# Moving the subtraction of the weights' low parts from GpSimd to VectorE in a two-block transformer kernel

## The reference, cut to what matters

```
h = rms_norm(x)
q, k, v, g_ret, x_lru, y_lru, gate_ret, gate_lru = split(h @ w_in)        # w_in is 1024 x 7168
o  = head_group_norm(retention(rotary(q), rotary(k), v))                  # 4 heads
ya = (o * silu(g_ret)) @ w_ret_o
xc = causal_conv4(x_lru)
hl = scan(a * h + b),  a, b from sigmoid(xc @ w_r), sigmoid(xc @ w_i)     # RG-LRU
yb = (hl * gelu(y_lru)) @ w_lru_o
x  = x + (sigmoid(gate_ret) * ya + sigmoid(gate_lru) * yb) @ w_out
gate, val = split(rms_norm(x) @ ffn_w_up)                                 # 2 x 3072
x  = x + (gelu(causal_conv3(gate)) * val) @ ffn_w_down
out = rms_norm(x)
```

## Time and profile before

| | |
|---|---|
| median of 3 runs | 982.43 us |
| profiled execution, first to last instruction | 979.2 us |
| mean granted TensorE clock | 0.982 |
| TensorE matmul busy | 907.7 us, 93% |
| weight load busy | 831.9 us, 85% |
| VectorE busy | 465.1 us, 47% |
| ScalarE busy | 370.2 us, 38% |
| GpSimd busy | 519.6 us, 53% |
| GpSimd's low parts | 632 instructions, 481.3 us |
| VectorE's low parts | 10 instructions, 14.0 us |

### The profile page before, as it was taken

How to read it: one execution, slowest core, us unless ns; L and a number is a source line. 1 busy time by engine, 2 the same in 40 slices (tenths; PEclk the granted TensorE clock), 3 DMA queues, 4 the chain that set the end, 5 groups by cost and what they waited for, 6 DMA issues and landing times.

```text
span 979.2 us, 15689 instructions
## 1 busy us (share of the span) xinstructions
PE 907.7 (93%) x6134; PEld 831.9 (85%) x6134; DVE 465.1 (47%) x957; ACT 370.2 (38%) x678; POOL 519.6 (53%) x658
## 2 busy tenths in 40 slices
PE   5798998999999999999999999799999998999995
PEld 5797887888888776788989999798988998899894
DVE  4774577613588788712693266301112353232132
ACT  4345554212101144604344774253112343443441
POOL 4567562100011000203899589993340798999992
PEclk9899999999999899999999999899999999999999
DMA  9353330443443611221645344452623365555551
GB/s 348 99 167 121 111 130 31 167 146 131 132 169 130 258 44 45 86 102 29 229 152 159 121 179 145 145 178 100 223 65 129 109 192 156 189 179 189 179 186 44
DMA packets 37785, 139.38 MB, mean 142 GB/s; under 512 B 4304, under 2 KB 4432, under 8 KB 37456
## 3 DMA queue, kind: packets, MB, share of 16 engines
q1 hardware_dynamic: 37424, 136.90, 41.6%
q10 hardware_dynamic: 288, 1.48, 0.4%
HBM read 137.32 MB, written 1.05 MB: 141 GB/s over the span
## 4 chain that ended last, share of the span: by engine, by line
PE 49%; POOL 25%; DVE 11%; issue 9%; ACT 3%; DMA 2%; SPq 0%; DVEq 0%; ACTq 0%; POOLq 0%
POOL w_lo L2182 24%; PE psum L530 21%; PE psum L531 8%; PE psum L532 7%; PE psum L533 7%; DMA early<-in_early 2%; POOL rstd L2189 1%; PE psum L681 1%; DVE y_lo L1483 1%; PE psum L663 1%; ACT logits L1165 1%; DVE h_rows L1640 1%; PE psum L605 1%; PE psum L798 1%; DVE neg_max L1741 1%
## 5 line engine op out<-in xcount | busy, mean ns | idle before, releaser
L2182 POOL TENSOR_TENSOR w_lo<-raw,w_hi 128x256 fp32r<-128x256 f32 x632 | 481.3, 803 | 114.5 <-ACT w_hi L1077 112.4
L530 PE MATMUL psum<-first 128*128 128x256 f32 (+1 forms) x960 | 214.4, 380 | 4.9 <-ACT first L1115 2.2
L2189 POOL TENSOR_TENSOR rstd<-mean_sq,minus_half 128x8 f32<-128x8 f32 (+4 forms) x21 | 38.0, 1809 | 340.2 <-DVE mean_sq L1500 340.2
L1077 ACT ACTIVATE w_hi<-raw 128x1024 fp32r<-128x1024 f32 x168 | 172.1, 1055 | 111.8 <-DMA raw<-in_blocks 83.9
L531 PE MATMUL psum<-h_hi,w_hi 128*128 128x256 f32 x704 | 202.4, 288 | 12.8 <-POOL w_lo L2182 11.1
L530 PEld LDWEIGHTS psum<-first 128*128 128x128 f32 x960 | 178.1, 191 | 30.1 <-ACT first L1115 2.6
L532 PE MATMUL psum<-h_lo,w_hi 128*128 128x256 f32 x704 | 200.9, 285 | 0.0
L533 PE MATMUL psum<-h_hi,w_lo 128*128 128x256 f32 x704 | 200.8, 285 | 0.0
L531 PEld LDWEIGHTS psum<-h_hi,w_hi 128*128 128x128 f32 x704 | 136.9, 194 | 15.7 <-issue 14.3
L532 PEld LDWEIGHTS psum<-h_lo,w_hi 128*128 128x128 f32 x704 | 137.0, 195 | 0.1
L533 PEld LDWEIGHTS psum<-h_hi,w_lo 128*128 128x128 f32 x704 | 136.8, 194 | 0.0
(11 more groups left out here) (266 smaller groups left out, 1108.2 us busy)
## 6 DMA issues: line engine op xcount, KB each, us to landing
raw<-in_blocks SPq DMA_DIRECT2D x168, 512.0 KB, 3.5
first<-in_blocks SPq DMA_DIRECT2D x64, 512.0 KB, 4.4
w_late<-in_blocks SPq DMA_DIRECT2D x20, 512.0 KB, 4.4
early<-in_early SPq DMA_DIRECT2D x1, 1579.0 KB, 14.8
attention<-in_late ACTq DMA_DIRECT2D x1, 1376.0 KB, 6.9
rows<-in_mem SPq DMA_DIRECT2D x2, 512.0 KB, 4.4
x<-in_x SPq DMA_DIRECT2D x1, 1024.0 KB, 8.5
out_x<-h_rows SPq DMA_DIRECT2D x2, 512.0 KB, 2.6
```

The source lines that it names most:

```text
L530: return nc.tensor.matmul(out, lhs[0], rhs[0], start=start, stop=stop, skip_group_check=shared_bank)
L1077: nc.scalar.activation(split_part(w_hi, q), raw[:, q % RAW_SLOTS, :], ACT.Copy).then_inc(w_hi_ready, 1)
L2182: ins = nc.gpsimd.tensor_tensor(lo[:, at], full[:, at], hi[:, at].bitcast(F32), ALU.subtract)
L2189: rstd_ready.mark(nc.gpsimd.tensor_tensor(rstd[:, n % 2, 0:width], mean_sq[:, n % 2, 0:width], minus_half[:, 0:width], ALU.pow), name, pool)
```

## The change

VectorE takes the low parts of all halves from index 19 on, each in two instructions of 1024 columns. To do so, `split_to` on VectorE calls `own_low_parts` where it only counted before. Three calls of `split_to` in its program are added or moved, and GpSimd's wait for `head_centred` goes. GpSimd keeps the low parts of twelve halves of layer 0, of halves 16, 17 and 18, and all roots.

```diff
-VECTOR_LO = [("b_k", 1), ("m_qg0", 0), ("m_qg0", 1), ("b_v", 1), HALVES[-1]]
+VECTOR_FROM = len(L0_SPLIT) + SPLIT_SLOTS
+VECTOR_LO = [("b_k", 1), ("m_qg0", 0), ("m_qg0", 1), ("b_v", 1)] + HALVES[VECTOR_FROM:]
...
             def split_to(n):
 
-                split[0] = max(split[0], min(n, len(HALVES)))
+                while split[0] < min(n, len(HALVES)):
+                    j = split[0]
+                    split[0] += 1
+                    if j >= VECTOR_FROM:
+                        own_low_parts(HALVES[j])
...
             link(ins)
+            split_to(proj.after[("r_v1", 1)] + LEAD)
             for f in range(KT):
                 ins = V.tensor_tensor_scan(xc(f), tile_of(0, f), tile_of(3072, f), 0.0, ALU.mult, ALU.add)
...
             retention_gate(1, 1)
-            split_to(proj.after[("g_ret0", 1)] + LEAD + 2)
-            r = scale_from("gn", sumsq[:, 0:T * RET_HEADS], S)
+            mean_from("gn", sumsq[:, 0:T * RET_HEADS], S, 1.0)
+            split_to(proj.after[("gate_r0", 0)] + LEAD)
+            r = root_of("gn", P)
...
             link(ins)
+            split_to(proj.after[("gate_r0", 1)] + LEAD)
             normed.mark(V.tensor_tensor(h_rows[:, :, :], h_rows[:, :, :], rows[:, :, 2048:3072], ALU.mult), "g_ret", vec)
...
             split_to(len(HALVES))
-            own_low_parts(HALVES[-1])
...
                     for q in (2 * j, 2 * j + 1):
-                        if q == 2 * half_index[("gate_r0", 0)] + 1:
-
-                            pool.wait_ge(head_centred, 1)
                         pool.wait_ge(w_hi_ready, q + 1)
```

## The result

The changed kernel takes 959.62 us (median of 4 runs, 959.36 to 959.67) against 982.42 us (980.4 to 983.42): ratio 0.9769, interval 0.9756 to 0.9783. The forecast was 961.7 us, with a range of 957 to 973. The profiled execution took 959.64 us and its span is 957.8, 1.8 us less.

What follows compares the result with a forecast made beforehand. TensorE, busy 93%, was taken to lose 21.8 us in block 2, nearly all behind GpSimd's subtractions. Gains 5.3 + 8.8 + 6.6 = 20.7 gave span 958.5, plus 3.2 to the median: 961.7 us, range 957 to 973.

Steps and rivals of the forecast that it cites:

- A: Block 2, c16 to c26: takes 68.8 us where 11 halves need 63.5; 5.3 us back.
- FFN: Block 2's FFN, 759.5 to 970.25 us: takes 210.75 us where matmuls need 204.1; 6.6 us back.
- the scan: VectorE's eight scans in B, left at their old duration, 8.7 us; at 0.48 each, 5.4 us less.
- B: Block 2, c31 to c43 with retention matmuls: takes 91.3 us for 81.4; 8.8 back, 9.9 less 1.1.
- new stop: In B after c33: TensorE wants `decayed(2)` at 590.25 us, VectorE ends it at 591.4; 1.1 us lost.
- the root of the group norm: GpSimd's root beside `lo(38)` in B: could wait for two VectorE subtractions, 2.4 us, leaving the sum the same.
- Retention as VectorE's chain: Rival in B: low parts before tight banks and slow centring make banks late; B gives back 4, 966.5 us; chance 0.20.
- The FFN loop: Rival: convolution, GELU, high and low part pace the FFN; each step stops 0.9 us or more, 967 us; chance 0.08.
- The loads: Rival: landing of `raw` loads, not low parts, sets the stops; only the FFN gains, 975.8 us; chance 0.04.
- Slower, the convolution slow of itself: Rival: block convolution stays 13.2 us, low parts 1.5 each; A loses 15.9, FFN gains nothing, 993 us; chance 0.06.
- TensorE quicker in `down`: Rival in the FFN: 5% of the 0.2275 us matmul step is GpSimd's doing; 3.3 us more, 958.4; chance 0.05.
- GpSimd's pause: At 605.81 us in GpSimd's queue: listed among what goes with its subtractions from half 19 on, without a price.

Runs made afterwards that it cites:

- E5: Changed kernel plus two idle GpSimd subtractions of 256 columns, reading SBUF, for each quarter VectorE now does; 979.09 us, ratio 0.9963.
- E6: Changed kernel plus six idle GpSimd memsets of 256 columns, only writing SBUF, for each quarter VectorE now does; 959.66 us, ratio 0.9763.
- E10: Kernel before the change, with only GpSimd's wait for `head_centred` taken out; 986.23 us, ratio 1.0047.
- E3: Changed kernel with VectorE's low parts in four instructions of 256 columns a quarter instead of one of 1024; 960.35 us, ratio 0.9769.
- E9: Kernel before the change, GpSimd's low parts in one instruction of 1024 columns a quarter instead of four of 256; 990.1 us, ratio 1.008.
- E7: Changed kernel with the low parts of halves 19 to 47 given back to GpSimd, VectorE starting at the FFN; 977.82 us, ratio 0.9957.

## Why the prediction was right, and where it was off

**The mechanism and two of three stages.** A was to give back 5.3 us and gave 5.4, the FFN 6.6 and gave 7.0. `lo(19)` was to be done by 476 and the first convolution by 484.8; they ended at 476.7 and 485.3 in a stage that began 1.0 later. The low part was priced at 1.2 us and takes 1.22, the convolution at 0.48 and takes 0.477, centring at 1.25 and takes 1.23. The margin in a steady FFN step was to be 1.1 us and came out at 1.5.

**The term that was mis-sized: the scan.** B was to give back 8.8 us, 9.9 less a new stop of 1.1 at `decayed(2)`. It gave 9.9: the stop did not come. Eight scans had been priced at 8.7 us and took 4.76; `decayed(2)` began at 587.43, not at 590.8. I had read the narrow spread of the eight durations (1143 to 1170 ns) as a sign that GpSimd had no part in them. E5 and E6 decide it: beside GpSimd's reads the scan is 1148 ns, beside its writes 669. A steady loss can give a steady duration too; that it was so even because GpSimd's stream had no gaps and a fixed pace fits the rows, but was not tried on its own.

The Trainium skill (SBUF — State Buffer, Who interferes with whom) had said so: two inputs in SBUF on VectorE, a read of SBUF on GpSimd, and the two exclude each other. By that rule the stop is absent and the forecast 960.6. I had weighed the rule against the row and believed the row; E5 and E6 bear the rule out, for the scan as well. On the same ground it had put a price on the root of the group norm beside `lo(38)`, 2.4 us at most. The root took 2.68 us there, and 1.64 in E10, where no low part of VectorE stood beside it: 1.0 more, of which VectorE waited 0.39 and TensorE nothing, as the sum had it.

**The arithmetic.** The sum of the stages came out 0.7 us low: 0.1 (A), 1.1 (B), 0.4 (FFN), 0.1 (the stretch between), less 1.0 for layers 0 and 1. The last term is no effect of the change: nothing there is edited, and the profiles of the experiments scatter more than that. That it takes back nearly all of the 1.1 us by which B was mis-sized is chance. The other 1.4 us of the 2.1 between 961.7 and 959.62 are the step from span to median, taken as 3.2 and measured as 1.8. The 3.2 had set one execution's span against the median of others. In every execution on record for which both are known, the time stands 1.7 to 2.1 us above its own span, so the profile of before was, by my estimate from these steps, of one that took about 981.0. The right step for an execution was 1.8; what was left, 1.4, is where that execution lay among its kind, as E3's profiled execution lies 2.8 above its median.

**The rivals.**
1. *Retention as VectorE's chain*: no. Centring, squares and sums take 1.22 to 1.23 us each, as the factor in the earlier trace rows had it. The margins were thin all the same: with GpSimd reading (E5) TensorE waited 2.7 us for one gate there.
2. *The FFN loop*: no stop in any step. E3 shows where it would start: 0.41 us more a half bring one stop of 1.5 us.
3. *The loads*: refuted. ScalarE's waits for `raw` fell with the low parts (from 79.5 us in 39 waits to 15.8 in 6 in block 2), since SP's loads wait for these.
4. *Slower, the convolution slow of itself*: refuted by the 477 ns. What would have made it true is GpSimd's company, and E5 is the nearest case, with the convolution at 0.90 us: 979.1, back at the kernel before but not slower.
5. *TensorE quicker in `down`*: refuted. With GpSimd idle, four steps of 512 columns (830.64 to 831.55) still take 0.2275 us each:

```profile
830.64 0.39 PE L532 MATMUL psum<-w_hi,y_hi 128*128 128x512 f32 x1
...
831.55 0.39 PE L533 MATMUL psum<-w_lo,y_hi 128*128 128x512 f32 x1
```

**What the prediction had not seen.** It took the removal of GpSimd's pause as a part of what goes, at no price. E10 shows that the edit alone costs 4 us. And it took the loss behind GpSimd as one with its company: E9 shows the two apart. A quicker GpSimd gives A's matmuls and the FFN all of their time back, and the kernel loses more than that elsewhere, behind VectorE as far as it was traced. What stays open: why VectorE gets in between two GpSimd instructions in some places (0.95 us) and not in others (11.45 us) was not tried.

## What to carry to other kernels

While GpSimd streamed reads of SBUF here, a VectorE instruction with two inputs in SBUF took longer by about what GpSimd's running instruction can have left, or by far more; so price both engines' work again when it moves, since giving VectorE more work can cost it less. Before calling a duration an instruction's own, look for the same form beside an idle GpSimd; an even duration proves nothing. A wait in the queue of the engine that disturbs may be what lets the other one in: don't remove it alone. And when a median moves, compare the profiles stage by stage: E9 is slower as a whole and faster in the stages that it was meant for.

## What the runs showed of the hardware

- A VectorE instruction held off for as long as GpSimd's queue ran on: 10.98 us (E7) and 11.45 us (E10) for one that takes 1.23 us alone.
- Wide instructions on GpSimd are quicker per column (2.41 us for 1024, against 4 of 0.72) and worse for its neighbour (convolution 2.50 us instead of 0.95).
- GpSimd's memsets, 780 of 0.31 us, changed none of the VectorE lines shown (E6).
- The scan of 256 columns takes 0.667 us and follows the last by 0.6; beside GpSimd's reads (E5) it takes 1.148.
- Two inputs in SBUF are not the only case: the norm's diagonal, one input and a scalar for each partition, takes 0.73 us an instruction beside GpSimd's low parts and 0.24 without (1.46 and 0.48 for two), and in E9 two take 4.70. The convolution's first instruction, of the same kind, fell from 0.826 to 0.407 us with the change, but has 0.405 in E5; what decides between them is open.
- After the stop of 8.92 us in E7 the first matmul stands for 0.58 us and the next two follow each other by 0.22 instead of 0.12; the granted clock is 0.50 from 619.9 to 623.0 us, that is TensorE at 1.2 GHz, as after the stops in the earlier trace rows.
